# First modulation in two feature halves, x loaded ahead of it, and the first projection run over half of its depth in between

## The reference

```python
def modulate(h, shift, scale):
    return h * (1.0 + scale) + shift
...
        m_lat = jnp.split((cond_lat @ mod_w[layer] + mod_b[layer])[:, None, :], 6, axis=-1)
        m_ctx = jnp.split((cond_ctx @ mod_w[layer] + mod_b[layer])[None, None, :], 6, axis=-1)
        h_lat = modulate(rms_norm(x, norm_g[layer, 0]), m_lat[0], m_lat[1])
        h_ctx = modulate(rms_norm(ctx, norm_g[layer, 0]), m_ctx[0], m_ctx[1])
```

## Time and profile before

| | us |
|---|---|
| median of 3 runs | 2665.92 (2665.0 to 2668.69) |
| the profiled execution | 2670.28 |
| its span in the trace | 2668.5 |
| PE busy | 2564.5 (96%) |
| DVE busy | 1508.1 (57%) |
| ACT busy | 646.7 (24%) |
| HBM read | 383.08 MB |

### The profile page before, as it was taken

One profiled execution on the slowest core, in us unless ns is written; L12 is line 12 of the kernel. 1 busy time (PEld: TensorE's weight loads), 2 busy tenths in 40 slices (PEclk: granted clock), 3 DMA queues, 4 the chain that ended last, 5 costly groups with the idle time before them and its releaser, 6 DMA issues.

```text
span 2668.5 us, 38231 instructions
## 1 busy us (share of the span) xinstructions
PE 2564.5 (96%) x15612; PEld 1940.1 (73%) x15612; DVE 1508.1 (57%) x2963; ACT 646.7 (24%) x1707; POOL 0.2 (0%) x4
## 2 busy tenths in 40 slices
PE   6999799999999999999999999999999999999999
PEld 2545457888887864589996845658997864667999
DVE  4866657655777543116663764425774664433785
ACT  3145412111102110112202152232321134232320
POOL 0000000000000000000000000000000000000000
PEclk9999899999999999999999999999999999999999
DMA  8522115555574674235653433124564343114663
GB/s 333 202 83 52 37 32 158 158 174 174 197 276 158 254 282 174 94 110 159 162 175 127 158 87 104 64 95 135 166 193 144 127 126 95 64 65 134 167 176 125
DMA packets 335210, 386.59 MB, mean 145 GB/s; under 512 B 11052, under 2 KB 264124, under 8 KB 322748
## 3 DMA queue, kind: packets, MB, share of 16 engines
q1 hardware_dynamic: 332300, 378.15, 44.2%
q10 hardware_dynamic: 2736, 6.01, 0.6%
HBM read 383.08 MB, written 1.05 MB: 144 GB/s over the span
## 4 chain that ended last, share of the span: by engine, by line
PE 76%; DVE 11%; DMA 5%; issue 4%; ACT 3%; SPq 1%; ACTq 0%; DVEq 0%
PE acc L820 26%; PE acc L871 11%; PE mx L820 10%; PE acc L859 7%; PE acc L885 6%; DMA mod_w<-in_w_ada 2%; PE acc L901 2%; PE acc L1129 2%; DVE arena L2395 2%; PE acc L1178 2%; DMA mod_w<-in_mod_w 1%; PE mx L1526 1%; DVE arena L3188 1%; DVE hT L2428 1%; PE mx L993 1%
## 5 line engine op out<-in xcount | busy, mean ns | idle before, releaser
L820 PE MATMUL acc<-arena 128*128 128x128 f32 (+1 forms) x2184 | 353.1, 304 | 3.4 <-DVE arena L2937 1.0
L820 PEld LDWEIGHTS acc<-arena 128*128 128x128 f32 x2184 | 306.7, 191 | 22.1 <-ACT gate L2078 1.4
L871 PE MATMUL acc<-hT,ring 128*128 128x256 f32 (+1 forms) x1280 | 307.3, 402 | 2.2 <-ACT hT L1744 1.3
L871 PEld LDWEIGHTS acc<-hT,ring 128*128 128x128 f32 x1280 | 243.8, 191 | 64.1 <-issue 32.4
L2395 DVE SCALAR_TENSOR_TENSOR arena<-mod_w,vcols,arena 128x2048 f32<-128x2048 f32 x98 | 228.4, 2348 | 70.9 <-DMA mod_w<-in_w_ada 57.7
L859 PE MATMUL acc<-ring,hT 128*128 128x512 f32 x576 | 251.2, 596 | 5.9 <-ACT hT L1834 4.6
L885 PE MATMUL acc<-ring,hT 128*128 128x512 f32 x512 | 247.6, 605 | 0.7 <-ACT hT L1865 0.7
L859 PEld LDWEIGHTS acc<-ring,hT 128*128 128x128 f32 x576 | 109.3, 191 | 144.5 <-issue 139.3
L2753 DVE TENSOR_TENSOR arena<-ring 128x512 f32<-128x512 f32 (+1 forms) x136 | 91.8, 675 | 198.5 <-PE acc L820 182.5
L820 PE MATMUL acc<-hT,ring 128*128 128x128 f32 (+1 forms) x1208 | 187.0, 304 | 4.6 <-ACT hT L1834 2.2
L820 PE MATMUL acc<-arena,ring 128*128 128x128 f32 (+1 forms) x1160 | 182.9, 300 | 3.6 <-DVE arena L2804 2.0
(11 more groups left out here) (413 smaller groups left out, 3405.1 us busy)
## 6 DMA issues: line engine op xcount, KB each, us to landing
ring<-in_w_in SPq DMA_DIRECT2D x28, 2048.0 KB
mod_w<-in_w_ada SPq DMA_DIRECT2D x48, 1024.0 KB, 5.8
ring<-in_ffn_w_in SPq DMA_DIRECT2D x88, 512.0 KB
ring<-in_w_up SPq DMA_DIRECT2D x88, 512.0 KB
mod_w<-in_mod_w SPq DMA_DIRECT2D x40, 1024.0 KB, 5.0
ring<-in_odd_w_in SPq DMA_DIRECT2D x12, 2048.0 KB
ring<-in_ffn_w_out SPq DMA_DIRECT2D x16, 1024.0 KB
ring<-in_w_down SPq DMA_DIRECT2D x16, 1024.0 KB
```

The costliest lines, as they stand in the source:

```text
L820: ins = nc.tensor.matmul(out, w[:, k, :], h[:, k, :], start=start and k == 0, stop=stop and k == n - 1, skip_group_check=more)
L871: ins = nc.tensor.matmul(b[:, 0:hi - lo], w[:, k, P * f:P * (f + 1)], hT[:, k, lo:hi], start=k == 0, stop=k == KD - 1)
```

## The change

The loads of `ctx` and `x` move from ACT's queue to the head of SP's. The first modulation is no longer loaded by depth but by features: half 0 is columns 0 to 511 and 1024 to 1535 (shift and scale of blocks 0 to 3), half 1 the others. Each half comes in two quarters of 2 MB (four k-blocks by 1024 columns); of half 1 the first quarter goes into `mod_w`, the buffer that the slabs use later, all others into the ring. PE multiplies a quarter with two column groups (`mod_half`). `even_q` is run as: first half of the depth (k 0 to 3) for token tiles 0 and 1, then half 1 of the modulation, then the first half of the depth for tiles 2 and 3, then the transposes of half 1, then the second half of the depth for all four. DVE and ACT treat blocks 4 to 7 after the columns of half 1. Slabs 0 and 1 wait until PE has used `mod_w` (`mod_b_used`).

```diff
     a = Plan()
+    a.free_jobs("xT", KD)
     a.slab_tiles("modA", 2)
-    a.free_jobs("xT", KD)
-    a.slab_tiles("modA2", 2)
     a.free_jobs("norm0", 1)
...
     tiles("even", (("even_q", [4]),))
+    a.slab_tiles("modB", 1)
     a.free_jobs("even_k", 4)
...
-    first = a.tile["even_q"]
+    first = a.tile["even_bi"] - 2
     a.slab_tile = [first] * 4 + [first + 2] * 6 + [first + 4] * 4 + [first + 8] * 2
...
                     if i >= 2:
                         sp.wait_ge(mod_used, i - 1)
+                    else:
+                        sp.wait_ge(mod_b_used, 1)
...
-            for t in range(4):
-                load(wcols(a["mod_w"][0], 0, 2048)[:, 2 * t:2 * t + 2, :])
+            for j, name in enumerate(("ctx", "x")):
+                sp.dma_start(x_tok[:, 2 * j:2 * j + 2, :], a[name][0].rearrange("(t p) d -> p t d", p=P)).then_inc(x_in, 16)
+
+            def mod_quarter(half, k):
+
+                return [wcols(a["mod_w"][0], lo + 512 * half, lo + 512 * half + 512)[:, k:k + 4, :] for lo in (0, 1024)]
+
+            for k in (0, 4):
+                load(*mod_quarter(0, k))
             ew = a["even_w_in"][0]
             load(wcols(ew, 0, 512))
+            for n, part in enumerate(mod_quarter(1, 0)):
+                sp.dma_start(mod_b_w[:, :, 512 * n:512 * n + 512], part).then_inc(mod_b_in, 16)
+            load(*mod_quarter(1, 4))
             sp.dma_start(ekv_w, wcols(ew, 512, 768)).then_inc(even_kv_in, 16)
...
+            def mod_half(w, half, first):
+
+                for k in range(4):
+                    for c in range(2):
+                        at = 64 * half + 32 * c
+                        ins = nc.tensor.matmul(mx[at:at + 32, 3, :], cond[:, first + k, :], w[:, k, 512 * c:512 * c + 512],
+                                               start=first + k == 0, stop=first + k == KD - 1, tile_position=(0, at))
                 return ins
...
+            for first in (0, 4):
+                mod_half(weights(1024, 4), 0, first).then_inc(w_part, 1)
             norm(0, 512, "norm0")
-            mod_turn()
+            pe.wait_ge(mod_a_sb, 1)
+            mod_half_turn(0).then_inc(mod_a_t, 1)
 
             stage("even_q")
-            by_token(BOTH, 512, where="even")
+            w = weights(512)
+            banks = [bank() for _ in BOTH]
...
+            for i in BOTH:
+                if i == 2:
+                    pe.wait_ge(mod_b_in, 32)
+                    mod_half(mod_b_w, 1, 0).then_inc(mod_b_used, 1)
+                    mod_half(weights(1024, 4), 1, 4).then_inc(w_part, 1)
+                q_half(i, 0)
+            pe.wait_ge(mod_sb, 1)
+            mod_half_turn(1).then_inc(mod_t, 1)
+            turned[0] += 1
+            for i in BOTH:
+                q_half(i, 4).then_inc(acc_full, 1)
+                mod_after("even")
...
-            for j, name in enumerate(("ctx", "x")):
-                act.dma_start(x_tok[:, 2 * j:2 * j + 2, :], a[name][0].rearrange("(t p) d -> p t d", p=P)).then_inc(x_in, 16)
```

More of the change, by code:

```diff
@@ L459, in first_then_second_block, with mod_halves @@
         mod_late = [view(19456, 2048), view(21504, 2048)]
+        def mod_halves(v, half):
+            return v.rearrange("p (g c q) -> p g c q", g=2, c=2)[:, :, half, :]
+        mod_b_w = mod_w[:, :, :].rearrange("p a b -> p (a b)").rearrange("p (k n) -> p k n", n=1024)
         def mod_acc(g, j):
@@ L587, in first_then_second_block @@
         mod_used, mod_red, mod_sb, mod_t, mod_c = sem("mod_slabs_used"), sem("mod_summed"), sem("mod_rows_sb"), sem("mod_cols_ps"), sem("mod_cols_sb")
+        mod_a_sb, mod_a_t, mod_a_c = sem("first_mod_rows_sb"), sem("first_mod_cols_ps"), sem("first_mod_cols_sb")
+        mod_b_in, mod_b_used = sem("second_mod_half_in"), sem("second_mod_half_used")
         out_stored = sem("out_stored")
@@ L607, in first_then_second_block @@
         acc_full, acc_a, acc_v = sem("acc_full"), sem("acc_emptied_by_scalar"), sem("acc_emptied_by_vector")
-        vcol_ps, vcol_sb, cond_e, cond_ready = sem("vcol_ps"), sem("vcol_sb"), sem("cond_e"), sem("cond_ready")
+        vcol_ps, vcol_sb, cond_ready = sem("vcol_ps"), sem("vcol_sb"), sem("cond_ready")
         dve_chain, act_chain = sem("dve_chain"), sem("act_chain")
-        setup_done = sem("setup_done")
         ang_ready, rope_ready = sem("ang_ready"), sem("rope_ready")
@@ L622, in first_then_second_block @@
         hg_osq, hg_ors, cat_ready = sem("hg_out_ss"), sem("hg_out_rs"), sem("cat_ready")
-        ff_silu = sem("ff_silu")
         ret_rope, ret_s, ret_p, ret_o, ret_rs, ret_n = (sem(f"ret_{n}") for n in (
             "roped", "scores", "weighted", "out_ps", "rstd", "normed"))
-        lcol_ps, lcol_sb = sem("layer_cols_ps"), sem("layer_cols_sb")
         dc_silu = sem("dn_silu")
@@ L918, in transposed, with mod_half_turn @@
                     ins.then_inc(acc_full, 1)
[L920 to L924, removed]
-                return ins
[L927 to L933, removed]
+            def mod_half(w, half, first):
[4 more added lines that the diff above has]
+                                               start=first + k == 0, stop=first + k == KD - 1, tile_position=(0, at))
+                return ins
+            def mod_half_turn(half):
+                rows = slice(64 * half, 64 * half + 64)
+                for q in range(4):
+                    ins = nc.tensor.transpose(mx[:, 2, P * q + 64 * half:P * q + 64 * half + 64],
+                                              mod_rows[rows, P * q:P * (q + 1)], ident[rows, rows])
+                return ins
             def mod_turn():
@@ L1026, in _ @@
             ins.then_inc(vcol_ps, 1)
-            pe.wait_ge(cond_ready, 1)
-            mod_tiles("modA", 0)
             stage("xT")
@@ L1031, in _, with q_half @@
             transposed(x_tok, BOTH)
-            mod_tiles("modA2", 4)
+            stage("modA")
+            pe.wait_ge(cond_ready, 1)
+            for first in (0, 4):
+                mod_half(weights(1024, 4), 0, first).then_inc(w_part, 1)
             norm(0, 512, "norm0")
-            mod_turn()
+            pe.wait_ge(mod_a_sb, 1)
+            mod_half_turn(0).then_inc(mod_a_t, 1)
             stage("even_q")
-            by_token(BOTH, 512, where="even")
+            w = weights(512)
+            banks = [bank() for _ in BOTH]
+            def q_half(i, first):
+                for k in range(first, first + 4):
+                    first_use(k)
+                    ins = nc.tensor.matmul(banks[i], hT[:, k, P * i:P * (i + 1)], w[:, k, :], start=k == 0, stop=k == KD - 1)
+                return ins
+            for i in BOTH:
[10 more added lines that the diff above has]
+                mod_after("even")
             pe.wait_ge(even_kv_in, 16)
@@ L1757, in emptied_by_vector, with mod_half_cols @@
                 act.wait_ge(acc_v, pl.emptied("V", pl.own[name_of(stage)][n - 1] + 1))
+            def mod_half_cols(half):
+                cols = mx[:, 2, :].rearrange("p (q c r) -> p c q r", q=4, c=4)
+                for j in range(2):
+                    ins = nc.scalar.activation(mod_halves(modc[:, 0, j, 0:16], half), cols[:, 2 * half:2 * half + 2, :, j],
+                                               ACT.Copy)
+                return ins
             def mod_rows_out(g):
@@ L1824, in inverse_rms, with shifted @@
                 nc.scalar.activation(n_rs[:, 0:width], n_sq[0][:, 0:width], ACT.Exp, scale=-0.5).then_inc(norm_rs, 1)
-            def shifted(use, width):
-                for n, k in enumerate(block_order(use)):
+            def shifted(use, width, part=range(KD)):
+                for n in part:
+                    k = block_order(use)[n]
                     act.wait_ge(norm_h, KD * use + n + 1)
@@ L1881, in _ @@
             stage("norm0")
-            act.wait_ge(w_part, 4)
-            mod_rows_out(0)
+            act.wait_ge(w_part, 2)
+            nc.scalar.activation(mod_rows[0:64, :], mx[0:64, 3, :], ACT.Copy).then_inc(mod_a_sb, 1)
             inverse_rms(512)
-            mod_turn()
-            shifted(0, 512)
+            act.wait_ge(mod_a_t, 1)
+            mod_half_cols(0).then_inc(mod_a_c, 1)
+            shifted(0, 512, range(4))
+            act.wait_ge(w_part, 3)
+            nc.scalar.activation(mod_rows[64:128, :], mx[64:128, 3, :], ACT.Copy).then_inc(mod_sb, 1)
+            act.wait_ge(mod_t, 1)
+            mod_half_cols(1).then_inc(mod_c, 1)
+            turned[0] += 1
+            shifted(0, 512, range(4, KD))
             act.dma_start(fconst[:, 2 * P:], a["const_f"][:, 2 * P:]).then_inc(const_in, 16)
@@ L2419, in add_square, with scaled_x @@
                 V.tensor_tensor(n_sum[:, 0:width], n_sum[:, 0:width], n_sq[f % 2][:, 0:width], ALU.add).then_inc(norm_add, 1)
-            def scaled_x(use, width):
+            def scaled_x(use, width, part=range(KD)):
                 dve.wait_ge(norm_rs, use + 1)
-                for k in block_order(use):
+                for n in part:
+                    k = block_order(use)[n]
```

(12 more changed lines are left out.)

## The result

| | before | after |
|---|---|---|
| median | 2665.49 (2665.0 to 2668.69, 4 runs) | 2693.1 (2690.43 to 2693.76, 4 runs) |
| the profiled execution | 2670.28 | 2690.43 |
| its span | 2668.5 | 2688.6 |
| PE busy | 2564.5 | 2573.0 |

The changed kernel is slower: the ratio is 1.0101, with a 95% interval of 1.0089 to 1.0113. The medians differ by 27.6 us, the two profiled executions by 20.2.

The account below looks back on a forecast made before the run. DVE's slab chain, without slack at the second sum, was taken as the bound; slab 2 22.0 us later gave 2670.3 + 22.0 = 2692.3 for the profiled execution, 2687.9 us for the median, range 2678 to 2697.

Parts of the forecast that it names:

- The third rival: Much slower: small rows held up behind x and modulation, opening not earlier, +25.5 us, 2691, or 2697; chance 0.10.
- The low bound: Whole kernel: modulation lands at 19.6, no slow clock, even_q ends at 66.6, slab 2 at 76.2; +16.9 to +12.9 us.
- The opening: Start to first projection: even_q starts at 30.2 us, 11.6 us earlier than before.
- the 32 turns and the one us of landing: Small rows and x taking turns on two queues: 32 turns of 0.18 us from 2.4 us; both land about 9.1.
- the 19.4 us for the bytes ahead of them: Loads for the first modulation half: weights 11.0 us, x 4.7, the rest 1.3; from 2.4 us this is 19.4, landed 20.6.
- PE's doubled modulation and `even_q`: On PE: a quarter costs 3.4 us, the modulation 13.7 instead of 6.9; even_q runs from 30.2 to 70.5.
- The pause: PE between the transposes of half 1 and even_q's second halves: 2.8 us with nothing else to do.
- SP's wait: SP's even_bi load waits for all of even_q until 70.5, slabs 2 to 5 behind it; slab 2 22.0 us later.
- Slabs 2 to 8: DVE's slab chain from slab 2 at 81.3 to the eighth slab's end at 114.0: 32.7 us, as before.
- The sums: PE's two mod_sum stages: the first waits 15.6 us for DVE, the second 4 to 7.
- Faster, since PE alone decides: Whole kernel: slab 2 comes early and PE carries the earlier start to the end, 2663.4 us; chance 0.04.
- the second rival: Slower by half: DVE's 8.9 us of slab waits vanish, the slab chain catches up, 2672 to 2679; chance 0.08.

Follow-up runs that it names:

- second execution of the changed kernel: The unaltered changed kernel profiled again in another series, on the same chip as the other two: 2691.6 us, ratio 1.01 against the kernel before.

## Why the prediction was right, point by point

It said 2687.9 us, 22.0 us more; it was 27.6 in the medians (2693.1), inside the range of 2678 to 2697. That range is 19 us wide. The point missed by 5.6 of 27.6 us, and terms that were off in both directions added up to it. The third rival, an opening that isn't earlier, had figures that lie nearer (a start of `even_q` at 33.6, its end at 74, 2691) for a reason that didn't hold: the rows landed at 10.64 and not at 14.4, and the last square ended at 23.8 and not at 27.5. (The low bound's end of `even_q`, 66.6, is 66.9 by its own terms.) The mechanism below, the wait for `even_q` with slab 2 behind it, is what the runs bear out.

- **The opening: direction right, one term too small.** Rows and x were due at 9.1; x landed at 9.4, the rows at 10.64 (no row showed the 32 turns and the one us of landing that stood in the sum for them). The second quarter was due at 20.6; its products began at 23.35 and ended at 27.0 instead of 24.1. The term at fault is the 19.4 us for the bytes ahead of them: 11.0 us for weights in 2 KB rows was taken from a stretch in which one queue ran alone. I had seen that the queues take turns packet by packet, but let that act on the small rows alone, not on the stream that they interrupt. Between 11 and 13 us the changed kernel's queues moved 296 and 295 packets, the one 0.58 MB and the other 0.08; the tiny packets had taken as many places as those of 2 KB. With these rows moved away, `even_q` starts where the sum had it: 30.08 against 30.2.
- **By the Trainium skill** ("DMA: Bandwidth & Descriptors", section "Queues, rings and completion order") an engine drains a packet of some 9 to 17 descriptors before it turns to the next queue, and the small rows would have stayed late. They came at 10.64, before at 14.46, and the equal counts repeat: this trace doesn't agree, as far as a packet of the profile is one descriptor. The rival's condition, rows as late as before, falls.
- **PE's doubled modulation and `even_q`: right.** The quarters of half 1 took 3.46 and 3.5 us each (41.70, 45.16 and 48.69 are their starts and what follows), priced at 3.4. From the first product to the last it was 40.0 us (32.97 to 73.0), predicted 40.3. The pause, 2.8 in the sum, was 2.74.
- **SP's wait: right, and shown** by adding it to the kernel before and by undoing it in the changed one. `even_bi` was issued right behind `even_q`, and slab 2 used 11.5 us later; the sum had 10.8, between bounds of 9.6 and 11.5, and the upper one it was.
- **Slabs 2 to 8: nearly right.** From slab 2 to the eighth it took 31.6 us, where I kept 32.7: slab 6 waited 3.27 us, not the 4.44 of the earlier trace rows.
- **The sums: right in place and size, low in what follows.** 15.22 us of waiting (predicted 15.6), then 5.63 (4 to 7). But the second `mod_sum` took 3.58 us for the 1.92 of the earlier trace rows, with a granted clock of 0.50 from 176 to 180 us, behind a pause. I had counted that cost only on the first sum, where it is hidden. Of its 1.7 us, 1.0 came back, as the scores then waited 0.35 us for the columns and not 1.39.

```profile
106.81 9.33 DVE L2451 SCALAR_TENSOR_TENSOR arena<-mod_w,vcols,arena 128x2048 f32<-128x2048 f32 x4 [3.27 <-DMA mod_w<-in_mod_w]
...
172.12 4.61 DVE L2451 SCALAR_TENSOR_TENSOR arena<-mod_w,vcols,arena 128x2048 f32<-128x2048 f32 x2 [1.51 <-DMA mod_w<-in_mod_w]
```

```profile
116.00:120.00 4.00, 3.80 (x17) 0.83 (x18) 3.86 (x6) 0.00 (x0) 0.00 (x0) 0.50 0.73 233
...
176.00:180.00 4.00, 3.21 (x16) 0.59 (x16) 3.38 (x5) 0.00 (x0) 0.00 (x0) 0.50 0.01 3
```

The account from 22.0 to 25.8: +2.5 from the late opening (`even_q` ends at 73.0, not 70.5), +0.7 for slab 2, −1.2 at slab 6, +1.1 between the two sums, where the last slab's transfer is now waited for 1.51 us, and +0.7 at the second sum and the scores. What the medians have beyond 25.8, up to 1.8 us, varies between executions: the second one has 27.8 in the same place.

- **Faster, since PE alone decides: fell**, and so did the rival in which the slab chain catches up by half. DVE still waited 8.9 us for the slabs' transfers after 42 us, as much as in the earlier trace rows, and 14.1 for the issue besides. The kernel with the last quarter outside the ring has the time of the second rival (2677.49, in 2672 to 2679), but not its mechanism: DVE still waits 7.5 us for transfers there. It is early because the wait for `even_q` is gone.

## What to carry to other kernels

A load is queued twice, in its data and in the queue that issues it: when a ring gains or loses one tile, look up for every later load which tile it takes, who releases that and when, and above all what is queued behind it. Starting a stage early gives nothing as long as another engine's chain ends last; here an opening in halves came with +27 us, or with about −3 when two quarters of the weights, the first slabs, the transposes and the small rows around it had been moved. And small transfers are held back, on another queue too, for the time in which a large stream must land, even if they are only kilobytes: here moving them brought the second quarter's products 2.9 us forward.

## What the runs showed of the hardware that I had not expected

- When SP's and ACT's queues both had packets, they moved like numbers of them, whatever the sizes: 95 and 94 in 2 us before (SP's of 8 KB), 296 and 295 in the changed kernel (SP's of 2 KB). With packets of 2 KB on the one and of at most 0.5 KB on the other, the larger stream fell from 0.75 MB to 0.45 MB in 2 us, and the engines were 79% busy, not 105%.
- The half clock after a pause of PE is not the same length in each execution: the second halves of `even_q`, 32 rows behind the same 2.74 us, took 14.00 us in the first execution of the changed kernel (granted clock 1.00 throughout), 15.70 with the quarter outside the ring (0.57 from 60 to 64 us) and 17.00 in the second execution of the changed kernel (0.50 there). Ahead of an in-order wait this is passed on: of 3.8 us at the end of `even_q`, 3.6 stood at the first sum and 1.95 at the scores.
- Behind the wait of 15.2 us the sixteen rows of a sum took 3.64 us (granted clock 0.50 from 116 to 120 us) where they take 1.92 without one.
